# Band masks in one product, transposed weights copied by ScalarE alone, and scan gates copied out of their bank first

## Time and profile before

| what | value |
|---|---|
| median of 3 runs | 3389.44 us (3384.95 to 3391.86) |
| the profiled execution: time, span | 3384.89 us, 3383.1 us |
| PE busy | 3103.9 us (92%) |
| DVE busy | 1915.5 us (57%) |
| ACT busy | 1179.9 us (35%) |
| POOL busy | 210.6 us (6%) |
| mean granted clock of TensorE | 0.964 |

### The profile page before, as it was taken

One profiled execution on the slowest core, in us unless ns is written; L12 is line 12 of the kernel. 1 busy time (PEld: TensorE's weight loads), 2 busy tenths in 40 slices (PEclk: granted clock), 3 DMA queues, 4 the chain that ended last, 5 costly groups with the idle time before them and its releaser, 6 DMA issues.

```text
span 3383.1 us, 43105 instructions
## 1 busy us (share of the span) xinstructions
PE 3103.9 (92%) x17878; PEld 2575.9 (76%) x17878; DVE 1915.5 (57%) x2796; ACT 1179.9 (35%) x1795; POOL 210.6 (6%) x138
## 2 busy tenths in 40 slices
PE   7998899999999788999989899988999998898898
PEld 6787778888887666788877788875788776776677
DVE  7776555656434674788543543557353645456655
ACT  4224341212223453322343333325222543433432
POOL 0003100000010000000000320000000203100000
PEclk9998899999999999999989999999999999999999
DMA  5554123333321002555431122200313222230123
GB/s 211 158 181 137 44 75 125 125 125 125 102 67 63 14 1 75 172 189 186 126 87 62 59 83 80 93 26 1 98 63 135 74 79 75 88 116 26 66 94 125
DMA packets 100091, 323.92 MB, mean 96 GB/s; under 512 B 14310, under 2 KB 20326, under 8 KB 98744
## 3 DMA queue, kind: packets, MB, share of 16 engines
q1 hardware_dynamic: 89812, 291.29, 26.6%
q10 hardware_dynamic: 10084, 29.87, 2.4%
HBM read 301.46 MB, written 19.66 MB: 95 GB/s over the span
## 4 chain that ended last, share of the span: by engine, by line
PE 78%; DVE 9%; ACT 7%; issue 4%; DMA 1%; POOL 1%; ACTq 0%; SPq 0%; DVEq 0%; POOLq 0%
PE PS L391 77%; ACT whi L198 1%; PE PS L394 1%; ACT Pq L1319 1%; DVE STs L1356 1%; DVE STq L1356 1%; DVE wlo L212 1%; ACT Ps L1319 1%; DMA Ht<-in_hT 1%; ACT nt L641 0%; ACT FS L1746 0%; POOL rows L2589 0%; POOL rows L2587 0%; DVE JUNK L544 0%; DVE mH L1158 0%
## 5 line engine op out<-in xcount | busy, mean ns | idle before, releaser
L391 PE MATMUL PS<-U,whi 128*128 128x512 f32 (+1 forms) x4992 | 1072.3, 364 | 77.5 <-DVE U L671 21.3
L391 PEld LDWEIGHTS PS<-U,whi 128*128 128x128 f32 x4992 | 844.9, 193 | 248.9 <-issue 42.9
L212 DVE TENSOR_TENSOR wlo<-stage,whi 128x1024 fp32r<-128x1024 f32 x339 | 427.1, 1262 | 966.8 <-ACT whi L198 966.3
L198 ACT ACTIVATE whi<-stage 128x1024 fp32r<-128x1024 f32 x339 | 357.8, 1057 | 1348.3 <-PE PS L391 1277.3
L391 PE MATMUL PS<-U,wlo 128*128 128x512 f32 (+1 forms) x2496 | 552.5, 355 | 0.0
L391 PE MATMUL PS<-Y,whi 128*128 128x512 f32 (+1 forms) x2240 | 506.1, 362 | 13.6 <-DVE Y L2236 4.5
L391 PEld LDWEIGHTS PS<-U,wlo 128*128 128x128 f32 x2496 | 419.4, 189 | 73.7
L391 PEld LDWEIGHTS PS<-Y,whi 128*128 128x128 f32 x2240 | 383.2, 190 | 87.7 <-issue 7.2
L391 PE MATMUL PS<-whi,U 128*128 128x512 f32 (+2 forms) x1152 | 323.1, 368 | 8.4 <-ACT g1qk L1773 1.9
L391 PE MATMUL PS<-Y,wlo 128*128 128x512 f32 (+1 forms) x1120 | 283.5, 360 | 0.0
L391 PEld LDWEIGHTS PS<-whi,U 128*128 128x128 f32 x1152 | 205.9, 189 | 51.0 <-issue 6.2
(11 more groups left out here) (432 smaller groups left out, 3114.0 us busy)
## 6 DMA issues: line engine op xcount, KB each, us to landing
stage<-in_w SPq DMA_DIRECT2D x128, 512.0 KB, 4.0
stage<-in_ada SPq DMA_DIRECT2D x80, 512.0 KB, 3.7
stage<-in_adb SPq DMA_DIRECT2D x48, 512.0 KB, 3.8
stage<-in_p_mg SPq DMA_DIRECT2D x16, 512.0 KB, 3.7
stage<-in_p_ma SPq DMA_DIRECT2D x16, 512.0 KB, 3.7
stage<-in_p_ms SPq DMA_DIRECT2D x16, 512.0 KB, 3.7
stage<-in_wo SPq DMA_DIRECT2D x16, 512.0 KB, 3.6
GS<-FS ACTq DMA_DIRECT2D x20, 384.0 KB
```

The source lines that it names most:

```text
L198: act.activation(self.parts[r % n][0], self.stage[i % len(self.stage)], ACT.Copy).then_inc(*self.S.up("w_hi", i))
L212: dve.tensor_tensor(lo, self.stage[i % len(self.stage)], hi.bitcast(F32), ALU.subtract).then_inc(*self.S.up("w_lo", i))
L391: return pe.matmul(o, l, r, start=start, stop=stop_, skip_group_check=True)
```

## The change

1. **Masks.** `sMR` becomes one row of 384 columns, left mask, zeros, right mask, and the identity gets its own tile `sID`. All masks of a tile of queries are added in one product over all its latent columns: 384 in the two middle tiles, 256 in the first and the last one (left mask and zeros, or zeros and right mask). So four products of 128 columns become two of 384, and two of 128 become two of 256. ScalarE prepares the masks in four instructions in place of two.
2. **Transposed weights.** ScalarE copies the columns beyond 512 too, in a second instruction right behind the first; VectorE's copy (L1374) and the event `a_ptd` are gone.
3. **Scan's gates.** When the projection is done, ScalarE copies it to `FS` at once, ahead of the rounding of the next weight tile (in the steps that are spilled the copy stays behind the rounding). The slot's `until` is now this copy (`g_raw`). Sigmoid then reads `FS`, and VectorE multiplies with `FS`. The copy waits for the spill of the step before, and the spill of the step after waits until VectorE has read `FS` (`BEHIND` maps a gate to the fill before it).

```diff
-                    for c, mask in masks:
+                    for c, n_, l, r in masks:
                         for s in ss:
-                            last = mm(pe, s[:, c:c + 128], mask[0], mask[1], False, True)
+                            last = mm(pe, s[:, c:c + n_], l, r, False, True)
...
                     pe.wait_ge(*at("a_pta", a.tag, i))
-                    if c > 512:
-                        pe.wait_ge(*at("a_ptd", a.tag, i))
...
-                    act.activation(a.PT[:, :, 0:c], A_TURN[:, :, 0:c], ACT.Copy).then_inc(*up("a_pta", a.tag, i))
+                    ins = act.activation(a.PT[:, :, 0:min(c, 512)], A_TURN[:, :, 0:min(c, 512)], ACT.Copy)
+                    if c > 512:
+                        ins = act.activation(a.PT[:, :, 512:c], A_REST[:, :, 0:c - 512], ACT.Copy)
+                    ins.then_inc(*up("a_pta", a.tag, i))
...
-                if 0 <= n - 1 < N and a.width(n - 1) > 512:
-                    i = n - 1
-                    c = a.width(i)
-                    dve.wait_ge(*at("a_t", a.tag, i))
-                    if i:
-                        dve.wait_ge(*at("a_o", a.tag, i - 1))
-                    dve.tensor_copy(a.PT[:, :, 512:c], A_REST[:, :, 0:c - 512]).then_inc(*up("a_ptd", a.tag, i))
...
-            act.activation(sMR[:, 0, :], IDENT, ACT.Copy).then_inc(*up("s_mask", 0))
-            act.activation(sMR[:, 1:3, :], CM[:, 384:640].rearrange("p (b e) -> p b e", b=2), ACT.Copy).then_inc(
-                *up("s_mask", 1))
+            act.activation(sID[:, :], IDENT, ACT.Copy).then_inc(*up("s_mask", 0))
+            act.activation(sMR[:, 0:128], BANDL, ACT.Copy).then_inc(*up("s_mask", 1))
+            act.activation(sMR[:, 128:256], IDENT, ACT.Copy, scale=0.0).then_inc(*up("s_mask", 2))
+            act.activation(sMR[:, 256:384], BANDR, ACT.Copy).then_inc(*up("s_mask", 3))
...
-            pe_proj(pe, T(name + str(L), j), xU, L == 0, ("g_gate", L, j) if n is None else ("fill", L, n))
+            pe_proj(pe, T(name + str(L), j), xU, L == 0, ("g_raw", L, j) if n is None else ("fill", L, n))
...
-            W.hi(act, i)
-            act.wait_ge(*at("w_used", i))
             if n is None:
-                act.activation(GL[L].G[j // 2][j % 2][:, 0:N], B.of(i)[:, 0:N], ACT.Sigmoid).then_inc(*up("g_sig", L, j))
+                act.wait_ge(*at("w_used", i))
+                act.wait_ge(*at("spill", L, BEHIND[j]))
+                act.activation(FS[:, 0:N], B.of(i)[:, 0:N], ACT.Copy).then_inc(*up("g_raw", L, j))
+                W.hi(act, i)
+                act.wait_ge(*at("g_raw", L, j))
+                act.activation(GL[L].G[j // 2][j % 2][:, 0:N], FS[:, 0:N], ACT.Sigmoid).then_inc(*up("g_sig", L, j))
             else:
+                W.hi(act, i)
+                act.wait_ge(*at("w_used", i))
...
+                for k, last in BEHIND.items():
+                    if last == n - 1:
+                        act.wait_ge(*at("g_gate", L, k))
...
-                dve.tensor_tensor(y, y, B.of(i)[:, 0:N], ALU.mult).then_inc(*up("g_gate", L, j))
+                dve.tensor_tensor(y, y, FS[:, 0:N], ALU.mult).then_inc(*up("g_gate", L, j))
```

More of the change, by code:

```diff
@@ L50 @@
     "y_hi": ("f_hi", "s_yhi", "g_yhi", "q_yhi", "v_yhi"), "y_lo": ("f_lo", "s_ylo", "g_ylo", "q_ylo", "v_y"),
-    "h_new": ("res", "b_add", "e_r", "h_final"), "evicted": ("m_qk", "s_qk", "q_z", "fill", "g_qk", "g_af", "v_x"),
+    "h_new": ("res", "b_add", "e_r", "h_final"), "evicted": ("m_qk", "s_qk", "q_z", "fill", "g_raw", "g_qk", "g_af", "v_x"),
     "modulated": ("n_mul", "u_mod"), "gain": ("n_gain", "u_gain"), "rows_act": ("m_va", "g_va"),
@@ L229, in scan_steps @@
     early = [(tag, j) for tag in "gas" for j in range(8)]
-    tiles, gates = {}, {}
+    tiles, gates, behind = {}, {}, {}
     for place in places:
@@ L233, in scan_steps @@
             tiles[place] = ("p_gg", 2 * place[1] + place[2] // 4, None)
+            behind[tiles[place][1]] = len(gates) - 1
         else:
@@ L238, in scan_steps @@
             tiles[place] = ("p_m" + tag, j, n)
-    return tiles, gates
-STEPS, EARLY = scan_steps()
+    return tiles, gates, behind
+STEPS, EARLY, BEHIND = scan_steps()
 def weight_plan():
@@ L1293, in pe_attention @@
                         pe.wait_ge(*at("a_pta", a.tag, i - 1))
-                        if a.width(i - 1) > 512:
-                            pe.wait_ge(*at("a_ptd", a.tag, i - 1))
                     else:
@@ L1303, in pe_attention @@
                     last.then_inc(*up("a_t", a.tag, i))
-            wide_ones = [i for i in range(N) if a.width(i) > 512]
             B.until[4:6] = [(("a_pta", a.tag, N - 1),)] * 2
-            B.until[6:8] = [(freed(N // 4 - 1), ("a_ptd", a.tag, wide_ones[-1]))] * 2
+            B.until[6:8] = [(freed(N // 4 - 1), ("a_pta", a.tag, N - 1))] * 2
             B.n = 0
@@ L1325, in act_attention @@
                     i = n - 1
-                    c = min(a.width(i), 512)
+                    c = a.width(i)
                     act.wait_ge(*at("a_t", a.tag, i))
@@ L1400, in trunk_kernel @@
         sScr = [wide(f"sr{i}", offY + 2048 * i, 512) for i in range(2)]
-        sMR = place("sMR", [128, 3, 128], F32R, offZ + 33408)
+        sID = place("sID", [128, 128], F32R, offZ + 33408)
+        sMR = place("sMR", [128, 384], F32R, offZ + 33920)
         sTiles = []
@@ L1404, in trunk_kernel @@
             first, last_ = max(j_ - 1, 0), min(j_ + 2, 4)
-            sTiles.append((128 * j_, [(128 * first, 128 * (last_ - first)), (512, 256)],
-                           ([(0, (sMR[:, 0, :], sMR[:, 1, :]))] if j_ else [])
-                           + ([(128 * (last_ - first - 1), (sMR[:, 0, :], sMR[:, 2, :]))] if j_ < 3 else [])))
+            n_ = 128 * (last_ - first)
+            o_ = 0 if j_ else 128
+            sTiles.append((128 * j_, [(128 * first, n_), (512, 256)], [(0, n_, sID[:, :], sMR[:, o_:o_ + n_])]))
         SWA = Attention("s", offU, 2, sTiles,
@@ L1426, in pe_swa @@
             pe_rows(pe, "sv", [T("sv", u) for u in range(2)], xU, 6, 256, lambda j: (("s_v", 2 * j + 1),))
-            pe_attention(pe, SWA, [("r_done", "s", 9), ("s_v", 5), ("s_mask", 1)], lambda m: ("s_ylo", m))
+            pe_attention(pe, SWA, [("r_done", "s", 9), ("s_v", 5), ("s_mask", 3)], lambda m: ("s_ylo", m))
             pe_out(pe, "sout", ("s",), xY, False, [("s_ylo", 7)] * 8)
```

## The result

The changed kernel takes 3369.11 us (median of 8 runs, 3363.22 to 3381.93) against 3389.57 us (8 runs, 3384.47 to 3393.38): ratio 0.9948, 95% interval 0.9932 to 0.9964. So it is faster by 0.52%, 17.6 us at the ratio (the two medians are 20.5 us apart), where I had forecast 30.7 us and a range up to 3371. On the forecast's own baseline the ratio gives 3389.44 x 0.9948 = 3371.8 us: at the upper edge of the range, just outside. The direction was right, the size was not, and some 13 us by the ratio, 10 by the medians, are to be found.

A forecast was written before the change was run, and what follows sets the result against it. The prediction took TensorE, with its waits at the scans' gates, as the bound. Gates -32.8, masks -1.2 and copies +3.3 gave -30.7 us from the 3389.44 median: 3358.7 us, own range 3351 to 3366, wider range 3348 to 3371.

The forecast's parts named there:

- The stops at the gates, -32.8 us: In both layers' scans, TensorE's stops at eight gates go: 17.2 us plus 15.6 us, of which 22.1 are waits, the rest clock.
- The bank free before the level ends, nothing late next: In the scans, ScalarE's copy ends inside the level; the next factor keeps 0.8 us margin in layer 1; cost nothing.
- The rival of two longer table switches: In the scans, longer ScalarE table switches make the next level's factor late, some +10 us: 3368 us; chance 0.06.
- The masks, -1.2 us: Wider mask products end 0.1 us earlier in 12 of 16 wide jobs: 1.2 us gained, bounds 0 and 2.4.
- The copies, +3.3 us: ScalarE's second copy delays rounding in `finish`: 0.35 us at 6 grouped-attention and 0.3 at 4 sliding-mixer places; bounds 0 and 5.8.
- The clock some stretches more or less elsewhere: Behind the scans, the shift in time throws the clock anew; with masks and copies it gives the range 3351 to 3366 us.
- gates that gain, but attention that loses through a few falls of the clock: Rival: the gates gain, but 6 falls of clock in the attention cost +9 us: 3367 us; chance 0.07.
- The clock falls anyway: Rival: in the scans the low clock comes at another point, so only waits of 22.1 us are gained: 3369 us; chance 0.12.

The follow-up runs named there:

- the gates alone: Only the scan's gate edit, masks and transposed weights as before, against the kernel before: 3367.47 us, ratio 0.9939.
- the copies alone: Only ScalarE's copies of the transposed weights, against the kernel before: 3391.54 us, ratio 1.0006.
- the masks alone: Only the mask edit, against the kernel before: 3384.79 us, ratio 0.9986.
- the second trace of the changed kernel: The whole change timed and profiled once more, against the kernel before: 3368.71 us, ratio 0.9943.
- the six stretches without a stop: Both layers of three kernels with values' products moved behind the gate projections: gates with wide masks 3353.64 us, whole change 3355.13, kernel before 3384.02.
- the whole change: All three parts, with the values' products also moved behind the gate projections, against the kernel before: 3355.13 us, ratio 0.9903, range 3347.23 to 3363.59.
- 1.2 us of work added: Kernel before plus 5 repeated 512-column products ahead of layer 1's values' products, against the kernel before: 3398.87 us, ratio 1.0033.
- 2.3 us of work added to another: Changed kernel plus 10 repeated products ahead of layer 1's values' products, against the kernel before: 3357.06 us, ratio 0.9903.

## Why the prediction was wrong

- **The stops at the gates, -32.8 us: right.** 31.1 us in the trace of the changed kernel, 31.4 with the gates alone. Both parts of it came: no wait, and the 5.53 us are 4.00. The two steps around a gate are 4.38 us shorter in layer 0 (4.30 forecast) and 4.34 in layer 1 (4.28). The missing 1.7 us are not in these steps. The scans hold low clock at other places: 8.8 us of it in all in layer 0 and 5.3 in layer 1, where it was 19.0 and 14.5. One of them is new, in the middle of layer 0's scan, at a projection without a stop, and costs 1.5 us. In the changed kernel's trace:

```profile
1972.46 5.51 PE L393 MATMUL PS<-U,whi 128*128 128x512 f32 x16
```

- **The bank free before the level ends, nothing late next: right.** The factor came 0.3 us earlier than reckoned, and no level waited. The rival of two longer table switches is out: the sigmoid starts 1.29 us behind the start of its load, as before. So the drain that the Trainium skill, "ScalarE: Activation LUTs", section "What ACT_TABLE_LOAD costs", adds to a switch of set does not show here either.
- **The masks, -1.2 us: wrong in sign by the traces, small.** +0.2 to +0.6 us. Two steps failed. I took it that 128 columns cost no less than 256; that holds in a stream, but in a group this short the first product's columns count: the second starts 0.16, 0.22 and 0.28 us behind the first at 128, 256 and 384 columns. And 384 columns saved 0.04 us, not 0.1, in each job: the second product starts 0.28 us behind the first, where I took 0.17. The 0.13 us that I read between products of 128 columns was a mean of 0.16 for the first and 0.11 for the others. The bounds given, 0 and 2.4, did not hold by the traces either. (The gap formula of the Trainium skill, "TensorE: Matmul & The Clock Gate", section "Back-to-back issue gap", would have given -1.3 us, with 162 ns at 384 columns where this trace has 0.28 us: it has no term for the start of a short group.)
- **The copies, +3.3 us: right in size.** 0.27 us at each `finish` for 0.35 and 0.30, +2.7 us; and 1.0 us that I had not seen, where layer 0's attention goes to jobs of 256 columns. Together 3.7 us. Ordinary jobs are unchanged at 4.97 us.
- **"The clock some stretches more or less elsewhere": the step that failed.** The sum has no term for it, and the range gave it, with masks and copies, about 7 us to either side; a fall was priced at 1.5 us, as at the gates. In the profiled execution one fall over the values' products of layer 1 cost 12.5 us, since the clock stayed down for 30.7 us in place of 3.4. It is in the traces of the changed kernel (both), of the gates alone and of the copies alone, and not in those of the kernel before and of the masks alone. The case was there as a rival, "gates that gain, but attention that loses through a few falls of the clock", at 0.07 and 3367 us. It was the right time for a near reason: one long fall ahead of the attention, not several short ones within it. I looked for falls where TensorE waits, not where it works without a gap on a long run of thin products and stays at the low clock. The forecast did say that the shift of everything behind the scans throws the clock anew; what it had wrong is how much one throw can cost.
- **"The clock falls anyway" in the scans: out but for one.** The falls of 3.4 us at seven of the eight gates went with the stops; the new one in layer 0 is shown above, and every trace with the gates' edit has it, 94 us behind the scan's first product.
- The rest of the difference between the two traces, 3.3 us ahead of any edit and 4.2 us in the sliding mixer (with 21.6 us of low clock in place of 12.3), does not come again: the second trace of the changed kernel has 0.9 us less than the kernel before up to the mixer's first query and 167.3 us for the mixer against 166.3.

What stays open: whether it takes both the stop and the thin products to bring the fall. No kernel had the stop filled and the products at the old place, so this is argued from the six stretches without a stop that did not fall; they may also have been aligned well. A stop and thin products do not suffice, as layer 0's stream shows. Open too: how often the kernel before has the fall, and why the masks alone measure 4 us faster than their trace says.

## What to carry to other kernels

A saved stop moves all that follows, and where the clock is near falling, the new alignment can give back two fifths of the gain (12.5 of 31.1 us) at a place that the change never touches. Look ahead of time for long runs of thin products behind a stop, try dense products in front of them, and compare edits once such places are out of the way: here that cut the execution-to-execution scatter of the kernel before from 16 us to 6, though the whole change kept 16. When a change yields less than its own stretch shows, time the stretches of both traces one by one before doubting the mechanism.

## What the runs showed of the hardware

- The clock's fall to 1.2 GHz came while TensorE was busy without a gap: it began 0.3 to 2.4 us into the 144 products of 128 columns, which stand behind a stop of 1.6 or 1.8 us. It lasted 30.7 or 34.1 us, until 3 to 4 us behind them, and doubled their time per product (16.3 us would be 32.6; 28.8 to 30.7 were taken, with the part ahead of the fall at full clock). Where it had not come within 2.4 us, the same products ran their 16.3 us at 2.4 GHz. So behind its first microseconds the stream kept the level that it had, in all these traces.
- 1.2 us of work added, in a kernel of 3388 us, cost 10 us; 2.3 us of work added to another saved 12.
- In a short group the second product starts 0.06 us later for every 128 columns that the first one has more: 0.16, 0.22 and 0.28 us at 128, 256 and 384 columns. A stream of 256-column products has 0.116 us from one to the next.
